# Second gate rows spread by TensorE, one expert's last loads issued ahead of the first gather, first refill in three parts

## The reference: one layer of a hybrid backbone with a mixture of experts

```python
x = x + g1 * (jnp.concatenate([attn, rec], axis=-1) @ lp['w_out'])
h2 = modulate(rms_norm(x, lp['norm2']), sh2, sc2)
x = x + g2 * moe(h2, ...)
# moe: best of 4 groups, then the best 2 of its 8 experts; 32 experts in all
hg = jnp.einsum('nd,edf->nef', x, w_gate)      # 1024 -> 256 for each expert
hu = jnp.einsum('nd,edf->nef', x, w_up)
act = jax.nn.silu(hg) * hu * combine[:, :, None]
y = jnp.einsum('nef,efd->nd', act, w_down)     # 256 -> 1024
```

## Time and profile before

| what | value |
|---|---|
| median of 3 runs | 628.58 us |
| profiled execution | 627.63 us, span 625.6 us |
| TensorE busy | 595.1 us (95%) |
| DVE busy | 352.2 us (56%) |
| ACT busy | 177.4 us (28%) |
| moved by DMA | 176.23 MB, mean 282 GB/s |
| SP's queue (q1) | 154.86 MB |
| mean granted clock of TensorE | 0.989 |

### The profile page before, as it was taken

One profiled execution on the slowest core, in us unless ns is written; L12 is line 12 of the kernel. 1 busy time (PEld: TensorE's weight loads), 2 busy tenths in 40 slices (PEclk: granted clock), 3 DMA queues, 4 the chain that ended last, 5 costly groups with the idle time before them and its releaser, 6 DMA issues.

```text
span 625.6 us, 9459 instructions
## 1 busy us (share of the span) xinstructions
PE 595.1 (95%) x3309; PEld 331.1 (53%) x3310; DVE 352.2 (56%) x788; ACT 177.4 (28%) x369; POOL 94.6 (15%) x131
## 2 busy tenths in 40 slices
PE   4999999999998999999999999999999999888987
PEld 1544555555565677645555545555555555445543
DVE  2745898765664987664666884334333433422446
ACT  4203887601144877731111101111111111111110
POOL 4000011121252000000000111122222212111200
PEclk9899999999999999999999999999999999988999
DMA  8999843330029628629213959999999999999978
GB/s 323 376 375 355 320 152 147 142 134 2 0 68 277 269 73 252 273 69 418 84 68 126 381 165 390 418 419 416 420 418 417 418 417 423 418 421 417 414 271 319
DMA packets 48273, 176.23 MB, mean 282 GB/s; under 512 B 10988, under 2 KB 18168, under 8 KB 34544
## 3 DMA queue, kind: packets, MB, share of 16 engines
q1 hardware_dynamic: 36992, 154.86, 63.5%
q0 software_dynamic: 6688, 15.58, 7.1%
q10 hardware_dynamic: 4560, 5.35, 2.4%
HBM read 163.31 MB, written 21.14 MB: 295 GB/s over the span
## 4 chain that ended last, share of the span: by engine, by line
PE 75%; DMA 13%; DVE 4%; SPq 4%; issue 1%; ACT 1%; ACTq 1%; POOL 1%; DVEq 0%; POOLq 0%
PE ps L1757 18%; PE ps L1574 11%; PE ps L1490 8%; PE ps L1773 8%; PE ps L1502 6%; DMA expert_w<-exp_w_up 5%; PE ps L1612 4%; PE ps L1639 4%; DMA gate_w<-lru_wx 3%; PE ps L1465 3%; PE ps L1621 3%; PE ps L1725 2%; SPq L358 2%; DMA recurrence<-w_mod 2%; PE ps L1411 1%; PE ps L1675 1%
## 5 line engine op out<-in xcount | busy, mean ns | idle before, releaser
L1757 PE MATMUL ps<-expert_w,hT_mixT 128*64 128x256 f32 x1120 | 136.4, 393 | 7.2 <-DMA expert_w<-exp_w_up 7.0
L1757 PEld LDWEIGHTS ps<-expert_w,hT_mixT 128*64 128x64 f32 x1120 | 84.0, 137 | 63.5 <-issue 19.5
L1490 PE MATMUL ps<-hT_mixT,w 128*128 128x128 f32 (+1 forms) x256 | 72.6, 437 | 1.2 <-DVE hT_mixT L918 1.2
L1574 PE MATMUL ps<-w,hT_mixT 128*128 128x512 f32 x160 | 71.9, 597 | 0.0
L1773 PE MATMUL ps<-expert_w,w 128*64 128x512 f32 x280 | 65.8, 598 | 0.0
L741 ACT ACTIVATE w<-ps 128x128 f32<-128x128 f32 x36 | 10.0, 278 | 188.6 <-PE ps L1757 188.6
L1490 PEld LDWEIGHTS ps<-hT_mixT,w 128*128 128x128 f32 x256 | 38.9, 191 | 35.8 <-issue 32.6
L1304 DVE SCALAR_TENSOR_TENSOR w<-w,ps 128x128 f32<-128x128 f32 x36 | 10.4, 288 | 82.3 <-ACT w L741 82.3
L1502 PE MATMUL ps<-w_qkv,hT_mixT 128*128 128x512 f32 (+1 forms) x160 | 53.2, 488 | 0.2 <-DVE v_tok L1006 0.2
L1322 DVE TENSOR_TENSOR w<-ps,w 128x1024 f32<-128x1024 f32 x17 | 20.8, 1225 | 56.5 <-PE ps L1773 56.5
L1574 PEld LDWEIGHTS ps<-w,hT_mixT 128*128 128x128 f32 x160 | 29.1, 191 | 29.9 <-issue 29.7
(11 more groups left out here) (289 smaller groups left out, 767.8 us busy)
## 6 DMA issues: line engine op xcount, KB each, us to landing
expert_w<-exp_w_down SPq DMA_DIRECT2D x31, 1024.0 KB
expert_w<-exp_w_gate SPq DMA_DIRECT2D x29, 1024.0 KB
expert_w<-exp_w_up SPq DMA_DIRECT2D x29, 1024.0 KB
w_mod_ring<-w_mod SPq DMA_DIRECT2D x14, 1024.0 KB, 6.5
y_rows<-zero_rows POOLq DMA_DIRECT2D x10, 512.0 KB, 9.2
expert_w<-y_rows SPq DMA_DIRECT2D x10, 512.0 KB, 6.9
recurrence<-w_mod SPq DMA_DIRECT2D x8, 512.0 KB, 10.0
w<-w_in SPq DMA_DIRECT2D x4, 1024.0 KB, 16.3
```

What stands on the lines that cost most here:

```text
L1490: ins = pe.matmul(ps[:, bank, 0:n], w1v[:, c, m * P:(m + 1) * P], HM[:, c, lo:lo + n], start=(c == 0), stop=(c == DC - 1))
L1574: ins = pe.matmul(ps[:, 2 * (t % 2) + half, :], HM[:, c, t * P:(t + 1) * P], w1v[:, c, half * 512:(half + 1) * 512], start=(c == 0), stop= ...
L1757: ins = pe.matmul(ps[r, 2 + k, 0:2 * P].rearrange("p (k f) -> p k f", k=2), xT[:, c, r], gate_up(i)[:, :, c, k:FF:FC], start=(c == 0), sto ...
```

## The change

Four things are changed.

1. g2 is loaded as two rows of 4 KB to one partition, ahead of expert 4's gate. TensorE multiplies each half of 512 columns by a row of ones on one partition into PSUM banks 0 to 3, which puts the row on all 128 partitions, and ACT copies it to `g2`. These four matmuls stand where `keep_clock(4)` stood.
2. Expert 5's down weights are issued behind `kept_down[0]` as soon as the context row of `bc` has been read (`scaled`). Its gate weights wait for the h2 stores (`last_rows`) in place of the first gather, which `kept_down[1]` now waits for.
3. The first refill goes in three parts, channels 0 to 1, 2 to 3 and 4 to 7 of each expert's 8, and TensorE does the gate and up matmuls of every step in these parts.
4. `keep_clock` writes to PSUM bank 6 before the steps, and two semaphores become one (`turn`).

```diff
 # SP
             sp.wait_ge(S["out_mm"], 2 * NT)
+            for i, v in enumerate((1, 0)):
+                sp.dma_start(g2[0:1, i, :], a["mod_rows"][v:v + 1, 5 * D:6 * D]).then_inc(S["g2_in"], 16)
             sp.dma_start(ring[:, HOME[4], 0:EW], wg_v[4]).then_inc(wgu_in[2], 16)
-            for i, v in enumerate((1, 0)):
-                sp.dma_start(g2[:, i, :], a["mod_rows"][v, 5 * D:6 * D].partition_broadcast(P)).then_inc(S["g2_in"], 16)
             sp.dma_start(kept_down[0], wd_v[KEPT, :, 0:D].rearrange("p (c n) -> p c n", c=DC)).then_inc(kept_in, 16)
+            sp.wait_ge(S["scaled"], 1)
+            w_down(sp, 5, 5)
             sp.wait_ge(S["h2"], NT)
             sp.wait_ge(S["lg_mm"], NT)
-            sp.wait_ge(S["xg_in"], 16)
+            sp.wait_ge(last_rows, 16)
             sp.dma_start(ring[:, HOME[5], 0:EW], wg_v[5]).then_inc(wgu_in[2], 16)
-            w_down(sp, 5, 5)
             sp.wait_ge(S["ssq2"], 2 * NT)
             sp.wait_ge(S["idx_mm"], 1)
+            sp.wait_ge(S["xg_in"], 16)
             sp.dma_start(kept_down[1], ...).then_inc(kept_in, 16)
...
+PARTS_OF_GU = ((0, DC // 4), (DC // 4, DC // 2), (DC // 2, DC))
-                for half in range(2):
-                    if half == 0:
-                        sp.wait_ge(S["gu_half"], done)
+                for part, (c0, c1) in enumerate(PARTS_OF_GU):
+                    if part < 2:
+                        sp.wait_ge(S[("gu_quarter", "gu_half")[part]], done)
                     else:
                         sp.wait_ge(S["gu_mm"], done * FC)
                     for j in range(2 * s, 2 * s + 2):
                         for src, lo in ((wg_v, 0), (wu_v, EW)):
-                            sp.dma_start(ring[:, HOME[j], lo + half * EW // 2:lo + (half + 1) * EW // 2], ...)
+                            sp.dma_start(ring[:, HOME[j], lo + c0 * FF:lo + c1 * FF],
+                                         src[q * 2 + (j - 2 * s), :, c0 * FF:c1 * FF])\
+                              .then_inc(wgu_in[s] if part == 2 else parts_in, 16)
 # ACT
+            def g2_rows(i):
+                for half in range(2):
+                    act.wait_ge(S["bias_mm"], 2 + 2 * i + half + 1)
+                    act.activation(g2[:, i, half * 512:(half + 1) * 512], ps[:, 2 * i + half, :], ACT.Copy).then_inc(S["prepared"], 1)
+            g2_rows(0)
             h2_out(NT - 1)
+            g2_rows(1)
 # DVE
-            dve.wait_ge(S["g2_in"], 16 * 2)
+            dve.wait_ge(S["prepared"], 9)
 # TensorE
-            pe.wait_ge(S["gated"], 2 * NT - 2)
+            pe.wait_ge(S["gated"], 2 * NT)
             pe.wait_ge(wgu_in[0], 64)
-            keep_clock(4)
+            pe.wait_ge(S["g2_in"], 16 * 2)
+            for i in range(2):
+                for half in range(2):
+                    pe.matmul(ps[:, 2 * i + half, :], ones[0:1, :], g2[0:1, i, half * 512:(half + 1) * 512], start=True, stop=True)\
+                      .then_inc(S["bias_mm"], 1)
             rank(NT - 1)
-            keep_clock(4)
+            keep_clock(4, 6)
...
             def x_in(n):
                 pe.wait_ge(S["xg_in"], 16 * (n + 1))
+                if isinstance(n, int):
+                    pe.wait_ge(S["prepared"], 9)
...
-                for half in range(2):
+                for part, (c0, c1) in enumerate(PARTS_OF_GU):
                     for k in range(FC):
-                        for c in range(half * DC // 2, (half + 1) * DC // 2):
+                        for c in range(c0, c1):
...
-                    if half == 0:
-                        ins.then_inc(S["gu_half"], 1)
+                    if part < 2:
+                        ins.then_inc(S[("gu_quarter", "gu_half")[part]], 1)
```

More of the change, by code:

```diff
@@ L241, in build @@
             "out_done v p act xg_in xt_mm gu_mm dn_mm xT_v xT_a th_ok act_ok aT_mm aT_ok y_v idxc_ok pidc_ok y_out "
-            "y_zero gu_half stepw w_mm now gsel chosen tail_mm fin sg_ok pool_turn sp_turn cache_out st_col st_t st_ev").split()}
+            "y_zero gu_quarter gu_half stepw w_mm now gsel chosen tail_mm fin sg_ok turn cache_out st_col st_t st_ev scaled").split()}
         rows_in = [sem(f"rows_in{i}") for i in range(NT)]
@@ L245, in build @@
         h2_at = [sem(f"h2_at{i}") for i in range(2)]
-        x1_at, last_rows, kept_in, halves_in = (sem(n) for n in ("x1_at", "last_rows", "kept_in", "halves_in"))
+        x1_at, last_rows, kept_in, parts_in = (sem(n) for n in ("x1_at", "last_rows", "kept_in", "parts_in"))
         wm_in = [sem(f"wm_in{i}") for i in range(6)]
@@ L484, in refill_in_halves @@
                     w_down(sp, q * 2 + (j - 2 * s), j)
-            refill_in_halves(HELD, 0)
+            refill_in_parts(HELD, 0)
             with sp.Fori(0, BODIES - 2) as it:
@@ L498, in _ @@
             sp.wait_ge(S["y_out"], 16 * steps)
-            sp.sem_inc(S["sp_turn"], 1)
+            sp.sem_inc(S["turn"], 1)
             for t in range(NT):
@@ L825, in step_of @@
                 pool.wait_ge(S["xt_mm"], n + 2)
-                pool.sem_inc(S["pool_turn"], 1)
+                pool.sem_inc(S["turn"], 1)
                 gather(idxc[:, 0:1])
@@ L1146, in scaled @@
                 dve.wait_ge(S["x1"], 2 * t + half + 1)
-                step(dve.tensor_tensor(h2_row(t)[:, 4 * half:4 * half + 4, :], x1_row(t)[:, 4 * half:4 * half + 4, :],
-                                       half_row(bc[:, t // LT, 1, :], half), ALU.mult))
+                ins = dve.tensor_tensor(h2_row(t)[:, 4 * half:4 * half + 4, :], x1_row(t)[:, 4 * half:4 * half + 4, :],
+                                        half_row(bc[:, t // LT, 1, :], half), ALU.mult)
+                if t == NT - 1 and half:
+                    ins.then_inc(S["scaled"], 1)
+                    dve.wait_ge(S["scaled"], 1)
+                else:
+                    step(ins)
             def h2(t, chunks, done):
@@ L1703, in _, with keep_clock @@
                 project(t, 1, range(5, DC))
-            def keep_clock(count):
+            def keep_clock(count, bank):
                 for _ in range(count):
-                    pe.matmul(ps[:, 3, :], ident[:, :], ring[:, HOME[0], 0:512], start=True, stop=True)
+                    pe.matmul(ps[:, bank, :], ident[:, :], ring[:, HOME[0], 0:512], start=True, stop=True)
             x1_turn(NT - 1, 1)
             logits(NT - 1)
-            pe.wait_ge(S["gated"], 2 * NT - 2)
+            pe.wait_ge(S["gated"], 2 * NT)
             pe.wait_ge(wgu_in[0], 64)
-            keep_clock(4)
+            pe.wait_ge(S["g2_in"], 16 * 2)
[3 more added lines that the diff above has]
+                      .then_inc(S["bias_mm"], 1)
             rank(NT - 1)
-            keep_clock(4)
+            keep_clock(4, 6)
             pe.wait_ge(S["slot"], TOP * NT + 1)
@@ L1758, in step_of @@
                                                 gate_up(i)[:, :, c, k:FF:FC], start=(c == 0), stop=(c == DC - 1))
-                        if half:
+                        if part == 2:
                             ins.then_inc(S["gu_mm"], 1)
-                    if half == 0:
-                        ins.then_inc(S["gu_half"], 1)
+                    if part < 2:
+                        ins.then_inc(S[("gu_quarter", "gu_half")[part]], 1)
                 act_in(n, 0)
@@ L1803, in _ @@
             pe.wait_ge(S["act_ok"], steps * FC + FC)
-            keep_clock(1)
+            keep_clock(1, 3)
             pe.wait_ge(S["chosen"], 1)
```

9 lines of the change are left out of this document (3 added, 6 removed).

## The result

The kernel with the change takes 633.06 us (median of 6 runs, 631.08 to 634.86), the one before 629.00 (6 runs, 627.99 to 630.43) beside it: ratio 1.0058, 95% interval 1.0034 to 1.0081. The forecast was 626.4, its range ended at 629.2. The profiled execution took 631.08, span 629.0 against 625.6.

The account below looks back on a forecast made before the run. The weight stream was taken to set the end. Of 5.0 us freed, 2.4 were lost at slot releases and 0.4 to the gate rows: 2.2 us sooner, 626.4 us median (625.4 profiled), range 624.0 to 629.2.

Parts of the forecast that it names:

- What bounds the kernel: Whole expert phase: the end is set by when the weight stream gets through, at 414 to 423 GB/s.
- (a): SP's queue before 364 us: small gate-row loads free 2.5 us of stream, filled by expert 5's down weights.
- (b): Expert 5's gate weights issued near 365.9 instead of 371.77, 2.5 us of stream; collision with the first gather costed at 0.
- Only 2.9 of the 5.0 us pass pair 4: Pair 4's refill, issued at 393.67 when TensorE frees its slot: 2.9 us of the freed stream get past it.
- Pair 9: Refill issued at 479.38 after a two-step pair: slack lets 2.2 to 2.9 us pass, 2.6 taken.
- one laggard: If the same DMA engine always lags, 2.7 us behind the mean at pair 12, more gain passes pair 9.
- (c): TensorE before the last `rank`: spreading matmuls take the same time; waiting for the small rows costs 0.4 us (0 to 1.0).
- (d): ACT's four added copies of 128x512, 0.60 us each, around the h2 store: cost 0.
- (e): First refill in quarters: worth 0 to 0.4 us, taken as 0; slow pieces cost 0.5, hidden by 1.7 us of room.
- (f): One semaphore for two, bank 6 for bank 3: 0; late waits at step 14 0 to 1.5, step 15 4 to 5 us.
- slower: Rival, chance 0.12: pair 3's quarter pieces load too slowly to finish before pair 4 may start; up to 2.3 us later, 630.9.
- Nothing left after pair 9: Rival, chance 0.24: little backlog remains at pair 9's release, so only 0.8 us sooner, 627.8.

Follow-up runs that it names:

- e12_late_cut: Kernel before with pair 10's down weights cut to their first 128 columns (two experts compute with old weights): 625.10 us, ratio 0.9936.
- e7_row128: Whole change, but g2 spread over 128 rows by a matrix with ones in its first row and zeros elsewhere: 629.81 us, 1.0027 against the kernel before.
- e9_row128_fill: Whole change with the 128-row zero-padded spread, plus two full clock-keeping matmuls in TensorE's wait for the last x1: 630.13 us, 1.0020 against the kernel before.
- e5_loads_only: Kernel before with only expert 5's loads moved earlier, g2 broadcasts left in the queue: 631.23 us, ratio 1.0061.
- e11_early_cut: Kernel before with pair 3's down weights cut to their first 128 columns (two experts compute with old weights): 628.20 us, ratio 0.9979.
- e10_row128_spread_only: Kernel before with only the g2 spread, done over 128 rows with zero padding, halves and old load order: 629.70 us, ratio 1.0005.
- e4_spread_only: Kernel before with only g2 spread by one-row matmuls, halves and old load order: 633.17 us, ratio 1.0059.
- e1_full: Changed kernel with the one-row spreading matmuls replaced by full ones on other data (g2 holds other numbers): 630.87 us, 1.0023 against the kernel before.
- e3_full_halves: Changed kernel with full matmuls for the one-row ones (g2 holds other numbers) and the first refill in halves: 629.59 us, 1.0010 against the kernel before.
- e2_halves: Changed kernel with the first refill in two halves as before: 632.37 us, 1.0038 against the kernel before.
- e6_quarters_only: Kernel before with only the first refill in three parts (quarter, quarter, half): 627.57 us, ratio 0.9997.
- c2_after: The changed kernel run once more, unchanged, for a second profile: 632.80 us.

## Why the prediction was wrong

**What bounds the kernel** held: `e12_late_cut` shows that the end follows the stream.

**(a), (b)** held as far as the issues go: the down weights left at 355.01, the gate weights at 365.86 (forecast 365.9), and the gather took 3.85 us as before. The collision that was costed at 0 stayed out, but by luck: the first gather started at 368.95, 3.09 us behind the issue, because TensorE's low clock had made the routing late. With the routing on time it costs 0.5 and 0.8 us (4.39 and 4.64 against 3.85, `e7_row128` and `e9_row128_fill`), and 1.7 where the broadcasts stay (`e5_loads_only`). The term should not have been 0.

**"Only 2.9 of the 5.0 us pass pair 4" failed**, and with it the whole gain of 2.2 us. The working let pair 3's pieces run without a hole from 376.6 to about 393, in time for pair 4 at 394.7. In fact the first quarter was issued at 376.94, not 375.6 (1.12 of that is the late train), and then the pieces were loaded at 152 and 271 GB/s up to 382. By the prediction's own way of counting, 283 GB/s from 371.5 to 394.79 are 6.6 MB of 7.4 issued, so pair 3 was through 2.0 us behind pair 4's release, near 396.8, and not before it could start (395.8). The same count puts it at 397.3 in the kernel before. So 0.5 us passed, not 2.9. The listed sign was there: at 392 to 396 after moved 426 GB/s, a full queue, where the slack of pair 4 should have shown. With the cut directly ahead of pair 4 (`e11_early_cut`) the slack does show, and 2.8 of the 2.9 us come out. The arithmetic of the narrow place was good; pair 3, in front of it, had been taken as free. That parts 2 and 3 bring nothing even with full rows is measured: `e7_row128` is 0.22% slower than `e10_row128_spread_only`, with an error of about 0.3, where the forecast had them 0.4% faster.

**Pair 9** (2.2 to 2.9 passing) can't be judged in the changed kernel, to which nothing much came. In `e11_early_cut` 1.8 of 2.8 passed, a little under the mean's 2.2: the "one laggard" that was to let 2.6 pass isn't supported.

**(c) "the same 128x512 shape out, so the same time" failed**, and it turned no gain into a loss. The wait for the rows was within its range (0.19 us, 0.77 in `e4_spread_only`, against 0 to 1.0), but the clock fell to 1.2 GHz among the one-row matmuls and stayed there, which the forecast had only as a mishap of 0.9 us. In four comparisons that differ in the rows alone (`e1_full` and `e7_row128` against the change, `e3_full_halves` against `e2_halves`, `e10_row128_spread_only` against `e4_spread_only`) the one-row kernel is slower by 0.35, 0.31, 0.28 and 0.54%. Only the last is clear of the noise by itself, and the change stands in two of them; their mean of 0.37%, 2.3 us, is more than half of the 0.58. The low clock is 22 us an execution in the one-row kernels, 13 to 15 in the others.
The Trainium skill (TensorE: Matmul & The Clock Gate, Part 1: The HAM clock gate) says that the clock follows how busy the array has been. Read as busy instructions this doesn't hold here: TensorE was busy for all of the 6.8 us from 358.5, at half the clock. The same page (Why this matters for your kernels) gives a matmul over 32 rows the time of one over 128. For the instruction itself the trace agrees: the shortest record of a one-row matmul took 587 ns, that of a full one 592. The cost fell on the clock, and with it on what came behind.

**(d)** 0: held; the store of h2 left at 361.32 us (361.43 before), and the first transposes waited for the gather alone. **(e)** Quarters against halves, 0: held (`e6_quarters_only`, 0.9997). The 0.5 us for slow pieces failed: its row, 354 GB/s, came from a full queue, and the change had emptied it. The 0.85 MB moved from 378 to 382 would take 2.0 us at 418 GB/s and took 4. Halves restarted as slowly (`e3_full_halves`), while loads of 1 MiB were at full rate some 2 us behind their issue (before: issue at 371.77, 422 GB/s from 374; after: issue at 365.86, 414 from 368). Whether pair 3 in whole loads would restart faster wasn't run, and why the pieces are slow stays open. **(f)**: step 14's wait of 1.46 us and step 15's of 5.28 were nearly forecast (0 to 1.5, 4 to 5). That a wait of 5.28 brings a longer low clock (9.52 for 8.83 us) was not.

The account in medians: forecast -0.35%, measured +0.58. The gain that didn't come is 0.35, the rows 0.37. What is left, 0.2%, is inside the intervals: the kernels with full rows lie between 1.0005 and 1.0027, and of the 0.2% that parts `e7_row128` from `e10_row128_spread_only` the slower gather shows 0.5 us, 0.1%; the rest stays open. So does the part behind step 15, where profiles of one kernel differ by 2 us.

The rival "slower" had the right sign and a part of the cause: pair 3 was not through when pair 4 could start. But its pieces cost it only the gain, halves would have done the same, and the loss came from the rows. "Nothing left after pair 9" put the loss at a later release than the one that took it.

## What to carry to other kernels

Freed transfer time is worth only what is left of it at each later place where the queue may run dry: go through the slot releases from the first one on, and ask at each what the engines would be loading just then, before counting the slack of a later one. A rate read from a full queue says little about one that has just been emptied. If a matmul also keeps the clock up, keep its rows when you give it work: pad a one-row matrix with rows of zeros. And when a load is moved ahead, see how close it comes to a small transfer on the critical path: a term that is 0 because another part is late comes back when that part is mended.

## What the runs showed of the hardware

- Among matmuls of float32 with one row in (1*128 by 1x512), back to back, TensorE's clock fell to 1.2 GHz and stayed there: granted 0.50 or 0.51 from 358.5 to 365.3 in all four profiles of such kernels, with TensorE busy all the time. With full matmuls in their place, or with 128 rows of which 127 of the matrix are zeros, it was 0.64 to 1.00 in twelve profiles. It can be low for a while with full ones too, so one profile doesn't tell.
- When the queue starts again after running dry the engines are slow as well as idle: between 378 and 380 after they were busy for 0.64 of the time and moved 152 GB/s, against 363 at a share of 1.02 before. With pieces of 256 KB (after) and 512 KB (`e3_full_halves`) full rate came back 4 to 7 us behind the first issue, with loads of 1 MiB some 2 us behind it. Why isn't known.
- A gather of 128 rows took longer the closer behind a load of 1 MiB it came:

| run | load issued ahead of the gather | gather |
|---|---|---|
| eight runs without such a load | | 3.68 to 3.92 us |
| `e2_halves`, `c2_after`, `e1_full`, the change, `e3_full_halves` | 5.77, 4.34, 3.26, 3.09, 2.66 us | 3.75, 3.71, 3.70, 3.85, 3.81 us |
| `e7_row128` | 1.86 us | 4.39 us |
| `e9_row128_fill` | 1.57 us | 4.64 us |
| `e5_loads_only` | 0.96 us | 5.42 us |
